# Retention projections that take x times the norm weight, with 1/rms multiplied in where their banks are read

## What is computed

```python
def rmsnorm(x, w):
    y = x * rsqrt(mean(x * x, axis=-1) + EPS)      # one factor per token: 1/rms
    return y * w                                   # one factor per column of x

h = rmsnorm(x, norm_w) @ w_in                      # 1024 -> 6144 columns
q, k, v, g = split(h)                              # 4 heads: 256 + 256 + 512 + 512 columns each
q = rotary(q); k = rotary(k) * DK ** -0.5
scores = einsum('bihd,bjhd->bhij', q, k) * decay
o = scores @ v + q_decayed @ S;  S_new = decay * S + k_decayed.T @ v
y = (rmsnorm_per_head(o) * silu(g)) @ w_out;  x = x + y
```

## Time and profile before

| | us |
|---|---|
| median of three runs | 537.3 |
| the profiled execution | 538.83 |
| its span, first to last instruction | 537.0 |
| PE busy | 525.5 (98%) |
| ScalarE, VectorE, GpSimd busy | 260.0, 319.5, 75.2 |
| DMA moved | 125.5 MB |

### The profile page before, as it was taken

How to read it: one execution, slowest core, us unless ns; L and a number is a source line. 1 busy time by engine, 2 the same in 40 slices (tenths; PEclk the granted TensorE clock), 3 DMA queues, 4 the chain that set the end, 5 groups by cost and what they waited for, 6 DMA issues and landing times.

```text
span 537.0 us, 9458 instructions
## 1 busy us (share of the span) xinstructions
PE 525.5 (98%) x3605; PEld 449.5 (84%) x3605; DVE 319.5 (59%) x581; ACT 260.0 (48%) x532; POOL 75.2 (14%) x84
## 2 busy tenths in 40 slices
PE   6899999999999999999999999999999999999997
PEld 5788977798878978798799999988877778999886
DVE  0874325872477625872489967845747665676631
ACT  5655533383336633383444546663535555655520
POOL 0283101720063101720000130000000000000000
PEclk9999999999999999999999999999999999999999
DMA  9676796999799996999826968407796737783211
GB/s 244 237 241 237 186 352 213 377 372 228 228 352 353 262 260 218 350 347 227 253 81 224 351 195 287 158 20 240 240 340 208 249 119 242 242 313 126 79 49 50
DMA packets 78832, 125.54 MB, mean 234 GB/s; under 512 B 3827, under 2 KB 41796, under 8 KB 78660
## 3 DMA queue, kind: packets, MB, share of 16 engines
q1 hardware_dynamic: 78706, 124.92, 73.1%
q10 hardware_dynamic: 82, 0.02, 0.0%
HBM read 98.97 MB, written 27.57 MB: 236 GB/s over the span
## 4 chain that ended last, share of the span: by engine, by line
PE 86%; DVE 7%; ACT 4%; DMA 2%; issue 1%; SPq 0%; DVEq 0%; ACTq 0%
PE bank L805 38%; PE bank L802 18%; PE bank L791 6%; PE bank L917 3%; DVE w_lo L1375 3%; PE bank L897 3%; PE bank L968 2%; DMA st<-in_x_sample 2%; PE bank L982 1%; PE bank L1029 1%; PE bank L931 1%; PE bank L888 1%; PE bank L875 1%; PE bank L817 1%; ACT w_hi L1090 1%
## 5 line engine op out<-in xcount | busy, mean ns | idle before, releaser
L1375 DVE TENSOR_TENSOR w_lo<-w_raw,w_hi 128x512 fp32r<-128x512 f32 x206 | 143.3, 731 | 114.4 <-ACT w_hi L1090 113.9
L1090 ACT ACTIVATE w_hi<-w_raw 128x512 fp32r<-128x512 f32 x208 | 119.1, 620 | 28.2 <-PE bank L805 15.1
L805 PE MATMUL bank<-xn_hi,w_hi 128*128 128x320 f32 x320 | 101.2, 320 | 2.6 <-DVE xn_lo L1386 2.6
L805 PE MATMUL bank<-xn_lo,w_hi 128*128 128x320 f32 x320 | 97.5, 309 | 0.0
L805 PE MATMUL bank<-xn_hi,w_lo 128*128 128x320 f32 x320 | 97.5, 309 | 0.0
L805 PEld LDWEIGHTS bank<-xn_hi,w_hi 128*128 128x128 f32 x320 | 59.6, 188 | 9.2 <-issue 6.1
L802 PE MATMUL bank<-w_hi,xn_hi 128*128 128x512 f32 x160 | 65.7, 411 | 0.0
L802 PE MATMUL bank<-w_lo,xn_hi 128*128 128x512 f32 x160 | 62.6, 391 | 0.0
L802 PE MATMUL bank<-w_hi,xn_lo 128*128 128x512 f32 x160 | 62.5, 390 | 0.0
L805 PE MATMUL bank<-ym_hi,w_hi 128*128 128x320 f32 x192 | 61.9, 322 | 0.0
L805 PEld LDWEIGHTS bank<-xn_lo,w_hi 128*128 128x128 f32 x320 | 59.8, 188 | 0.4
(11 more groups left out here) (215 smaller groups left out, 732.1 us busy)
## 6 DMA issues: line engine op xcount, KB each, us to landing
w_raw<-in_ret_w_in SPq DMA_DIRECT2D x24, 1024.0 KB, 9.8
st<-in_state_ret SPq DMA_DIRECT2D x32, 512.0 KB, 8.5
out_ret_state_sample<-st SPq DMA_DIRECT2D x32, 512.0 KB, 5.1
w_raw<-in_ret_w_out SPq DMA_DIRECT2D x8, 1024.0 KB, 9.2
w_raw<-in_moba_w_in SPq DMA_DIRECT2D x8, 1024.0 KB, 6.2
cache<-in_cache_k SPq DMA_DIRECT2D x16, 512.0 KB, 5.2
w_raw<-in_w_kv SPq DMA_DIRECT2D x8, 1024.0 KB, 5.8
cache<-in_cache_v SPq DMA_DIRECT2D x16, 512.0 KB, 4.5
```

The source lines that it names most:

```text
L805: mm = pe.matmul(bank[out][:, 0:T], w[:, wk, P * tile:P * tile + P], x[:, k, :], **flags)
L1090: act.activation(w_hi[:, c % 2, part], w_raw[:, c % RAW, part], ACT.Copy).then_inc(w_hi_done, 1)
L1375: dve.tensor_tensor(w_lo[:, c % 2, part], w_raw[:, c % RAW, part], w_hi[:, c % 2, part].bitcast(F32), ALU.subtract).then_inc(w_lo_done, 1)
```

## The change

- x times the norm weight, without 1/rms, is what is split into `xn_hi` and `xn_lo`. ACT makes `xn_hi` in one step with a scale per partition, for even slices from the bank, for odd ones from `xT`; DVE makes `xn_lo` from `xT` in one step. The copies to `xT` are shared: ACT the even slices, DVE the odd ones. The norm weights (`wcols`) are copied first of all.
- The sum of squares of the sample's rows, the roots, reciprocals and `diag` move behind slice 3. The product with ones becomes a step `RP` in the middle of chunk 0, into bank 3, and DVE copies it to the new tile `rin`. Twelve multiplications of zeros run in one piece before chunk 0.
- Readers of banks: DVE multiplies q, k and the gate by `rin` (L1494, L1501 of the changed kernel); ACT's SiLU then runs on `gs` in place; ACT's copies of v to `vp` and of `vs` to `vs_hi` take the token's 1/rms as scale; POOL multiplies `vs` by it before it subtracts; `s2` takes it as a factor.
- The first weight chunk comes as two transfers of 512 KB, and its first two pieces wait for the first alone. The transfer of `knw` moves behind the retention layer.

```diff
-        chunk("rq", h, 0, u[0:2] if h else [[], [("ST", 0)]])
+        chunk("rq", h, 0, u[0:2] if h else [([("RP",)], []), [("ST", 0)]])
...
+                if c == 0:
+                    sp.dma_start(to[:, 0:KT // 2], src[:, 0:KT // 2]).then_inc(first_w_loaded, 16)
+                    to, src = to[:, KT // 2:KT], src[:, KT // 2:KT]
+                sp.dma_start(to, src).then_inc(w_loaded[c % RAW], 16)
...
-                    pe.wait_ge(unsplit_done, 2)
...
-                    for n in range(6):
-                        pe.matmul(bank[7][:, 384:512], qz[:, 0:P], qz[:, 0:P], start=True, stop=True)
-                    pe.wait_ge(diag_done, 1)
-                    for t, (c0, m) in enumerate(TOK):
-                        mm = pe.matmul(bank[4 + t][:, 384:384 + m], ones[0:m, :], diag[0:m, t, 0:m], start=True, stop=True)
-                    mm.then_inc(rms_done, 1)
-                    for n in range(6):
+                    for n in range(12):
                         mm = pe.matmul(bank[7][:, 384:512], qz[:, 0:P], qz[:, 0:P], start=True, stop=True)
                     close(mm, 7)
+                elif kind == "RP":
+                    pe.wait_ge(diag_done, 1)
+                    await_free(pe, 3, *step)
+                    for t, (c0, m) in enumerate(TOK):
+                        mm = pe.matmul(bank[3][:, c0:c0 + m], ones[0:m, :], diag[0:m, t, 0:m], start=True, stop=True)
+                    close(mm, 3)
...
+                elif kind == "NORM":
+                    def scaled(kt):
+
+                        w = wcols[:, W_RET + kt:W_RET + kt + 1]
+                        if kt % 2:
+                            await_read(act, kt, "X", kt)
+                            act.activation(xn_hi[:, kt, 0:T], xT[:, kt, :], ACT.Copy, scale=w).then_inc(x_hi_done, 1)
+                            return
+                        await_full(act, kt, "X", kt)
+                        act.activation(xT[:, kt, :], bank[kt][:, 0:T], ACT.Copy).then_inc(bank_read[kt], 1)
+                        act.activation(xn_hi[:, kt, 0:T], bank[kt][:, 0:T], ACT.Copy, scale=w).then_inc(x_hi_done, 1)
...
-                        act.activation(vp[:, i, :], bank[b][:, :], ACT.Copy).then_inc(bank_read[b], 1)
+                        act.activation(vp[:, i, :], bank[b][:, :], ACT.Copy, scale=rms[:, i:i + 1]).then_inc(bank_read[b], 1)
...
-                        act.wait_ge(gated_done, h) if h else act.wait_ge(line_stored, 16)
-                        act.activation(gs[:, 2 * part + i, :], bank[b][:, 0:T], ACT.Silu).then_inc(bank_read[b], 1)
+                        await_read(act, b, *step[:3])
+                        act.activation(gs[:, 2 * part + i, :], gs[:, 2 * part + i, :], ACT.Silu).then_inc(silu_done, 1)
...
+                    def scaled_lo(kt):
+
+                        dve.wait_ge(x_hi_done, kt + 1)
+                        dve.scalar_tensor_tensor(xn_lo[:, kt, :], xT[:, kt, :], wcols[:, W_RET + kt:W_RET + kt + 1],
+                                                 xn_hi[:, kt, 0:T].bitcast(F32), ALU.mult, ALU.subtract).then_inc(x_lo_done, 1)
...
+                    elif what in ("rq", "rk"):
+                        qk = int(what == "rk")
+                        await_full(dve, b, *step[:3])
+                        if h:
+                            dve.wait_ge(rot_done, 2 * h - 1 + qk)
+                        dve.tensor_tensor(raw_qk[:, qk, i, :], bank[b][:, 0:T], rin[:, :], ALU.mult).then_inc(bank_read[b], 1)
+                    elif what == "rg":
+                        await_full(dve, b, *step[:3])
+                        if h == 0:
+                            dve.wait_ge(line_stored, 16)
+                        else:
+                            dve.wait_ge(gated_done, h)
+                        dve.tensor_tensor(gs[:, 2 * part + i, :], bank[b][:, 0:T], rin[:, :], ALU.mult).then_inc(bank_read[b], 1)
...
-                    pool.tensor_tensor(vs_lo[:, :], vs[:, :], vs_hi[:, :].bitcast(F32), ALU.subtract)\
+                    done(pool.tensor_scalar(vs_lo[:, :].bitcast(F32), vs[:, :], rms[0:TS, 2:3], None, ALU.mult))
+                    done.wait()
+                    pool.tensor_tensor(vs_lo[:, :], vs_lo[:, :].bitcast(F32), vs_hi[:, :].bitcast(F32), ALU.subtract)\
                         .then_inc(vs_lo_done, 1)
```

More of the change, by code:

```diff
@@ L387, in build @@
         small = mb("small", [P, 48])
+        knw = mb("knw", [P, HD])
         rsq, nmxs, dens = small[:, 0:20], small[:, 20:24], small[:, 24:28]
@@ L1159, in _ @@
                     flat = scr.ap().rearrange("p k t -> p (k t)")
-                    for t, (c0, m) in enumerate(TOK):
+                    for t in range(2):
                         act.wait_ge(x_loaded[t], 16)
-                        if t == 2:
-                            done.wait()
-                        done(act.activation(flat[0:m, D * (t % 2):D * (t % 2) + D], st[0:m, t, :], ACT.Square,
-                                            accum_out=rms[0:m, t:t + 1]))
+                        done(act.activation(flat[:, D * t:D * t + D], st[:, t, :], ACT.Square, accum_out=rms[:, t:t + 1]))
+                elif kind == "NORM":
[8 more added lines that the diff above has]
+                        act.activation(xn_hi[:, kt, 0:T], bank[kt][:, 0:T], ACT.Copy, scale=w).then_inc(x_hi_done, 1)
+                    act.wait_ge(wcols_done, 1)
+                    scaled(0)
+                    split_hi(0, 0)
+                    scaled(1)
+                    scaled(2)
+                    split_hi(0, 1)
+                    done.wait()
+                    act.wait_ge(x_loaded[2], 16)
+                    done(act.activation(flat[0:TS, 0:D], st[0:TS, 2, :], ACT.Square, accum_out=rms[0:TS, 2:3]))
+                    scaled(3)
                     done.wait()
@@ L1169, in _ @@
                         .then_inc(roots_done, 1)
[L1170 to L1186 removed]
+                    scaled(4)
+                    split_hi(0, 2)
+                    scaled(5)
+                    scaled(6)
+                    split_hi(0, 3)
+                    scaled(7)
                 elif kind == "TILE":
@@ L1411, in _ @@
                     ins.then_inc(diag_done, 1)
-                    await_full(dve, 3, "X", 3)
-                    done(dve.tensor_copy(wcols[:, 0:41], bank[3][:, 384:425]))
-                elif kind == "NORM":
-                    dve.wait_ge(rms_done, 1)
-                    for t, (c0, m) in enumerate(TOK):
-                        done(dve.tensor_copy(rsb[:, c0:c0 + m], bank[4 + t][:, 384:384 + m]))
-                    done.wait()
-                    for kt in range(KT):
-                        if kt < 3:
-                            await_read(dve, kt, "X", kt)
-                        else:
-                            await_full(dve, kt, "X", kt)
-                        normed(kt, W_RET, bank[kt][:, 0:T])
-                        if kt in (1, 3):
-                            split_lo(0, kt // 2)
-                        if kt:
-                            lower(kt - 1)
-                    lower(KT - 1)
+                    keep(7)
+                    for kt in range(4, KT):
+                        scaled_lo(kt)
+                elif kind == "RP":
+                    await_full(dve, 3, *step)
+                    dve.tensor_copy(rin[:, :], bank[3][:, 0:T]).then_inc(bank_read[3], 1)
+                    await_read(dve, 3, *step)
                 elif kind == "W":
@@ L1534, in _ @@
                     h = step[1]
-                    for i in range(4 * h, 4 * h + 4):
-                        await_read(dve, *tile_use("rg", i))
+                    dve.wait_ge(silu_done, 4 * h + 4)
                     dve.wait_ge(sq_done, h + 1)
```

72 lines of the change are left out of this document (38 added, 34 removed).

## The result

| | before | changed |
|---|---|---|
| median of the runs, us | 537.9 (4 runs, 536.5 to 539.6) | 545.4 (4 runs, 543.9 to 548.5) |
| the profiled execution | 538.8 | 548.5 |
| its span | 537.0 | 546.7 |
| TensorE's mean granted clock in it | 0.997 | 0.984 |
| PE busy in it | 525.5 | 532.8 |

The ratio is 1.0145, with a 95% interval from 1.0091 to 1.0200. The changed kernel is slower by 7.5 us; the forecast was 536.2 us with a range from 533.6 to 538.5.

What follows compares the result with a forecast made beforehand. PE's multiplications, plus what keeps PE from them at the start, were taken as the bound. Start −2.8 us plus 1.7 us lost in three heads gave −1.1 us: 536.2 us against the 537.3 median, range 533.6 to 538.5.

Steps and rivals of the forecast that it cites:

- SiLU starts there: First gate chunk, heads 1 to 3: SiLU starts at 118.4, after DVE's new bank read, instead of 115.14.
- POOL's two steps: Heads 1 to 3: multiplication (0.9 us) and subtraction on vs keep POOL until 115.25; DVE's norm ends at 116.8, not 115.65.
- Rival 2: Heads: POOL's multiplication takes 1.2 us or more, DVE's norm goes between, DVE only 0.1 late; 534.3 us, chance 0.10.
- From SiLU to the third low part: First gate chunk: SiLU's start to the end of the third low part, 3.2 us, or 3.4 with POOL's next step.
- the wait of a head: Heads 1 to 3, second gate chunk: PE waits 0.4 us for the third piece's low part at its thirteenth multiplication.
- The 0.15 us that I added for `sT`: Heads 1 to 3: DVE's second new read stands ahead of sT, which OP needs; 0.15 us more a head.
- The start: Up to the end of chunk 0: PE starts it at 15.75 and ends at 24.0, 2.8 us earlier than before.
- I let the clock fall always: Start: clock low from near 11.24 to 14.66, so PE's zeros run partly at 1.2 GHz and chunk 0 starts at 15.75.
- the hold of POOL in chunk 0: Chunk 0, slices 4 to 7: POOL's subtractions slow DVE's four subtractions; charged 0.35 us.
- the split of the first transfer: Start: half the first weight chunk comes sooner; costed at nothing, since PE cannot start then anyway.
- rival 4: Heads: rows of k come too late because ks_hi stands behind SiLU, so PE waits; 542 us, chance 0.08.
- the reads in `rq` and `rk` chunks: Each head's q and k bank reads moved to DVE: cost nothing, as PE needs the pieces a whole chunk later.

Runs made afterwards that it cites:

- e1: Changed kernel plus a one-column SiLU in heads 1 to 3, loading the function table ahead of ACT's wait for the first gate tile: 536.9 us.
- e3: Changed kernel with POOL's multiplication folded into ACT's copy and DVE's addition for vs (1/rms enters twice in the sample's scores times v): 538.4 us.
- e4: Changed kernel with SiLU of each head's first gate tile moved to the second, behind the KT reads and high parts of pieces 3 and 4: 534.1 us.
- e7: Kernel with that later SiLU, plus low parts of the first chunk's third and fourth pieces made by DVE instead of POOL: 532.9 us.

## Why the prediction was wrong

**The table load** is the step that failed. "SiLU starts there", at 118.4, holds only if the load has run while ACT waits; I took that for granted, and the load had no term in the sum. The bracket of the load at 116.66 above, 4.50 us for DVE's read, shows what I passed over. By ACT's list of waits all four such loads of the changed kernel waited for DVE's read, 15.2 us together; in e1 only that of head 0 did, which has no dummy ahead of it, for 1.4 us. SiLU has two waits in the code, and the load ahead of it carries that for DVE's read. The trace of before could not show it: by 113.85 everything that load or SiLU wait for there was fulfilled, so which wait the load carried is not seen. This cost 1.28 us a head, and e1 took it back.

**SiLU's start without it** was right: I said 118.4, in the coordinates of the trace of before. The load of the changed kernel starts at 116.66, and with its lead of 1.9 us that is 118.5. But the way there was another, and that the two ways cost the same is luck. I let POOL's two steps, the multiplication (0.9 us assumed, between 0.52 and 1.28 from the earlier trace rows; it measured 1.56) and the subtraction, hold DVE's norm until 115.25, for 1.1 us. They did not hold it; instead POOL's subtraction met the norm, moved behind it, and held the two low parts after it for 1.1 us. Rival 2 had the first half of this, and stopped one instruction too early: it took the subtraction to be put off without asking what DVE does next. Hence it missed the 1.1 us.

**From SiLU to the third low part** I forecast 3.2 to 3.4 us; from 117.95 to PE's start at 121.49 it is 3.5. So the wait of a head was forecast as 0.4 and measured 2.1 to 2.3: 1.3 of the difference is the load, the rest are tenths in that chain.

**The clock in the heads** had no term at all. I used the granted clock for the start alone. With 0.4 us of idle time that would have been right: with 0.6 (e1) and 1.2 (e3) no head lost it. With 1.9 us all three did, for 1.7 us each. A load of 1.3 us that was left out thus cost 3 us a head. The 0.15 us that I added for `sT` did not show: no wait for it is listed.

**The start** was right in size, in part by luck: −2.8 us, and e4, in which nothing else is left of the change, is 3.0 us below the kernel before, most executions having full clock there. In the profiled pair, with the clock down in both, it was −1.9, the forecast's lower end. Three terms in it were off. I let the clock fall always; where it stays up, the zeros take 2.7 us and chunk 0 starts at 12.7 to 13.2. I put the hold of POOL in chunk 0 at 0.35 us; it is 0.85 where the zeros end early (e4; e7 takes it away) and nothing in the profile of the changed kernel. And the split of the first transfer is worth 1.2 us, not nothing.

**What held**: no wait at `UP` (rival 4 was wrong in its mechanism, though its 542 us lay nearest); no loss in head 0, where the first `OP` comes 31.8 us after the two multiplications with `fin` (in chunk 1) in both kernels; nothing for `RP`, `knw`, or the reads in `rq` and `rk` chunks. With 3.0 from e4 the changed kernel adds up as 537.1 − 3.0 + 11.6 = 545.7 us, against 545.4 measured.

## What to carry to other kernels

When an operation's input moves to another engine, its table load can move behind the new wait, as here: look what the load itself waits for, also where the trace shows no wait because everything was already there, and put a load (by a one-column dummy) where the engine is idle. When a read of a bank goes to another engine, take the second step out of the queue's front as well, as e4 does. And price a wait of PE in two parts, its length and the clock behind it: here a wait of 2.1 to 2.3 us cost 3.9, and one of 0.6 us (e1) cost 0.9.
